# Scaling the attention's probabilities on ScalarE, and moving convolution taps from the V products into the first attention steps

## The reference, cut to what matters

```python
h = rms_norm_2(x, mix_norm_g[l])
u = h @ w_in[l]                                    # 512 columns for the convolution, then q, k, v
c = conformer_conv(conv_in, ...)                   # 31 taps by token, 256 channels
a = dilated_attention(qkv[0], qkv[1], qkv[2], positions)          # 12 heads of 64, 256 keys
mixed = jnp.concatenate([rms_norm_2(c, conv_out_g[l]), rms_norm_2(a, attn_out_g[l])], axis=-1)
x = x + mixed @ w_out[l]
x = x + memory_cross_attention(h, m, w_xq[l], w_xk[l], w_xv[l], w_xo[l])   # 4 heads of 256, 256 keys

def conformer_conv(conv_in, dw_w, dw_b, ln_g, ln_b):
    c = a * jax.nn.sigmoid(gate)
    c = <depthwise convolution with 31 taps>(c) + dw_b
    c = layer_norm(c, ln_g, ln_b)
    return jax.nn.silu(c)
```

## Time and profile before

| what | value |
|---|---|
| median of 3 runs | 2212.12 us (2212.11 to 2212.88) |
| the profiled execution | 2211.59 us, its span 2209.8 us |
| TensorE busy | 1968.7 us, 89% of the span |
| VectorE busy | 1119.8 us, 51% |
| ScalarE busy | 885.3 us, 40% |

### The profile page before, as it was taken

How to read it: one execution, slowest core, us unless ns; L and a number is a source line. 1 busy time by engine, 2 the same in 40 slices (tenths; PEclk the granted TensorE clock), 3 DMA queues, 4 the chain that set the end, 5 groups by cost and what they waited for, 6 DMA issues and landing times.

```text
span 2209.8 us, 33856 instructions
## 1 busy us (share of the span) xinstructions
PE 1968.7 (89%) x14272; PEld 1597.1 (72%) x14272; DVE 1119.8 (51%) x1832; ACT 885.3 (40%) x1504; POOL 16.9 (1%) x31
## 2 busy tenths in 40 slices
PE   6899889999999999989899999998899967667666
PEld 4787667777777877889599999897698754444443
DVE  2344656664887778447655566669665211101111
ACT  2423336554765667444444444643564200000001
POOL 0000000000000000000000000000000000000000
PEclk9899999999999999989999999999899988888898
DMA  7222005453455554224045445443134999999995
GB/s 271 82 77 80 16 6 178 150 184 110 153 181 181 191 177 162 90 69 168 3 155 189 156 159 178 162 156 127 48 117 175 416 420 421 420 419 420 420 420 241
DMA packets 90976, 428.00 MB, mean 194 GB/s; under 512 B 11073, under 2 KB 12610, under 8 KB 65858
## 3 DMA queue, kind: packets, MB, share of 16 engines
q1 hardware_dynamic: 78578, 379.03, 45.6%
q10 hardware_dynamic: 12240, 46.74, 6.2%
HBM read 424.68 MB, written 1.05 MB: 193 GB/s over the span
## 4 chain that ended last, share of the span: by engine, by line
PE 65%; DMA 18%; DVE 9%; ACT 6%; issue 2%; POOL 0%; SPq 0%; DVEq 0%; ACTq 0%
PE bank L458 42%; DMA area<-in_w 7%; PE bank L1532 7%; DMA ring<-in_w 4%; DMA his<-in_w 4%; DMA PPT<-in_w 2%; PE bank L482 2%; PE bank L2383 2%; PE bank L2339 2%; DVE ring_r L437 1%; DVE st L1239 1%; ACT his_r L429 1%; ACT PPT L1187 1%; ACT H L822 1%; PE bank L1170 1%
## 5 line engine op out<-in xcount | busy, mean ns | idle before, releaser
L458 PE MATMUL bank<-HH_r,his_r 128*128 128x256 f32 (+1 forms) x1568 | 532.9, 340 | 19.8 <-issue 9.5
L458 PE MATMUL bank<-HH_r,ring_r 128*128 128x256 f32 (+1 forms) x1568 | 518.5, 331 | 0.0
L437 DVE TENSOR_TENSOR ring_r<-ring,his_r 128x1024 fp32r<-128x1024 f32 x306 | 373.7, 1223 | 274.0 <-ACT his_r L429 272.9
L458 PE MATMUL bank<-H_r,his_r 128*128 128x256 f32 (+1 forms) x1504 | 499.2, 332 | 0.0
L429 ACT ACTIVATE his_r<-ring 128x1024 fp32r<-128x1024 f32 x306 | 323.3, 1058 | 405.9 <-PE bank L458 258.7
L458 PEld LDWEIGHTS bank<-HH_r,his_r 128*128 128x128 f32 x1568 | 298.2, 190 | 60.3 <-issue 16.0
L458 PEld LDWEIGHTS bank<-HH_r,ring_r 128*128 128x128 f32 x1568 | 298.2, 190 | 27.7
L458 PEld LDWEIGHTS bank<-H_r,his_r 128*128 128x128 f32 x1504 | 286.1, 190 | 30.8 <-issue 2.6
L2355 DVE TENSOR_TENSOR tmp<-tmp,bank 128x128 f32<-128x128 f32 x64 | 18.4, 287 | 382.3 <-ACT tmp L2348 265.0
L1532 PE MATMUL bank<-VT_r,his_r 128*128 128x512 f32 (+1 forms) x352 | 122.3, 348 | 9.5 <-DVE YF_r L1308 4.8
L2339 PE MATMUL bank<-area,KF 128*32 128x128 f32 x1888 | 88.2, 314 | 38.4 <-DMA area<-in_w 36.2
(11 more groups left out here) (393 smaller groups left out, 3259.6 us busy)
## 6 DMA issues: line engine op xcount, KB each, us to landing
area<-in_w SPq DMA_DIRECT2D x91, 1024.0 KB, 27.2
ring<-in_w_in SPq DMA_DIRECT2D x102, 512.0 KB, 3.5
ring<-in_w_gate_up SPq DMA_DIRECT2D x88, 512.0 KB, 3.5
ring<-in_w SPq DMA_DIRECT2D x36, 1024.0 KB, 27.4
HH<-in_w SPq DMA_DIRECT2D x26, 1024.0 KB, 27.2
ring<-in_w_down SPq DMA_DIRECT2D x44, 512.0 KB, 3.5
KX<-in_w_mod_rows ACTq DMA_DIRECT2D x28, 512.0 KB, 3.5
VX<-in_w_mod_rows ACTq DMA_DIRECT2D x28, 512.0 KB, 3.5
```

What stands on the lines that cost most here:

```text
L437: ve.eng.tensor_tensor(lo_slot(u), stream.slot(u), hi_slot(n).bitcast(F32), ALU.subtract).then_inc(*ve_lo.up(n))
L458: ins = pe.eng.matmul(out, a, b, start=k == 0 and m == 0, stop=end)
```

## The change

Five things change.

1. In attentions with `ahead=2`, ScalarE scales the probabilities of head h-1 by the reciprocal of their sum, behind the exponentials of head h. VectorE only makes the reciprocal. TensorE's turn waits for ScalarE.
2. The V products' units get one tap each (13 to 18), and steps 0 to 3 of the attention three each (19 to 30), ahead of the low part.
3. What follows the convolution stands two steps later: centre 4 and 5, affine 10, sigmoid 11, squares of the branch 11, its sums 12, its root 13. Its reciprocal stands in step 14, the spread and the gains behind the last step, in a call for h = 15.
4. ScalarE runs one small exponential before the attention.
5. The bank of the spread is given back in step 10, that of the branch after h = 15.

```diff
@@ -1153,7 +1153,7 @@
                             kc = 2 * j + cc_
                             for qb in range(2):
                                 i = qb if c.wide else 0
-                                pe.wait_ge(*ve_soft.at("p", c.site, g, i, c.n - 1))
+                                pe.wait_ge(*(ac_soft if c.ahead == 2 else ve_soft).at("p", c.site, g, i, c.n - 1))
                                 c0 = kc * P if c.wide else qb * 256 + kc * P
                                 ins = pe.eng.transpose(out[:, cc_ * 256 + qb * P:cc_ * 256 + (qb + 1) * P],
                                                        c.pps[slot * c.nq + i][:, c0:c0 + P], ident)
@@ -1187,6 +1187,13 @@
                             ac.eng.activation(p[:, m * w:(m + 1) * w], src[:, m * w:(m + 1) * w], ACT.Exp,
                                               bias=st[:, so + m:so + m + 1], scale=c.rq(h, i + m) if c.rq else 1.0,
                                               accum_out=st[:, so + 4 + m:so + 5 + m]).then_inc(*ac_soft.up("exp", c.site, h, i, m))
+                if c.ahead == 2 and 1 <= h <= c.nh:
+                    slot = (h - 1) % 3
+                    p, r = c.pps[slot], st[:, 8 * slot + 6:8 * slot + 8]
+                    ac.wait_ge(*ve_soft.at("inverse", c.site, h - 1, 0))
+                    for m in range(c.n):
+                        ac.eng.activation(p[:, m * 256:(m + 1) * 256], p[:, m * 256:(m + 1) * 256], ACT.Identity,
+                                          scale=r[:, m:m + 1]).then_inc(*ac_soft.up("p", c.site, h - 1, 0, m))
                 if 0 <= h - c.ahead < c.nh:
                     g = h - c.ahead
                     for j in range(c.nk // 2):
@@ -1216,6 +1223,8 @@
             p, so, w = c.pps[slot], 8 * slot, 512 // c.n
             ve.wait_ge(*ac_soft.at("exp", c.site, h, i, c.n - 1))
             ve.eng.reciprocal(st[:, so + 6:so + 6 + c.n], st[:, so + 4:so + 4 + c.n]).then_inc(*ve_soft.up("inverse", c.site, h, i))
+            if c.ahead == 2:
+                return
             ve.wait_ge(*ve_soft.last())
             for m in range(c.n):
                 ve.eng.tensor_scalar(p[:, m * w:(m + 1) * w], p[:, m * w:(m + 1) * w], st[:, so + 6 + m:so + 7 + m], None,
@@ -1813,7 +1822,7 @@
             for j in range(3):
                 for u in (16 + 2 * j, 17 + 2 * j):
                     ve_split(ve, two_on(unit("w_in_2", 0, 8 * u)))
-                    ve_conv_taps(ve, 2 * u - 19, 2 * u - 17)
+                    ve_conv_taps(ve, u - 3, u - 2)
 
 
         def ve_last_norm(ve, k):
@@ -1864,22 +1873,22 @@
                 if k == 7:
                     for tb in range(2):
                         banks.give("xv", half, tb)
-            if h == 2:
+            if h == 4:
                 out = banks.take((ve_taps, ("centered", 1)), "center")
                 pe.wait_ge(*banks.emptied("center"))
                 pe.wait_ge(*ve_taps.at("tap", 30, 1))
                 for j in range(2):
                     ins = pe.eng.matmul(out[:, 0:N], ones[:, :], CB[:, j, :], start=j == 0, stop=j == 1)
                 ins.then_inc(*pe_sums.up("center"))
-            if h in (4, 10):
-                site = "spread" if h == 4 else "branch"
+            if h in (6, 12):
+                site = "spread" if h == 6 else "branch"
                 pe_open(pe, site)
                 for n in range(2):
                     pe_sum(pe, site, n, 2, N)
-            if h in (7, 13):
-                pe_spread(pe, "spread" if h == 7 else "branch", N, give=False)
-            if h in (8, 14):
-                banks.give("sum", "spread" if h == 8 else "branch")
+            if h in (9, 15):
+                pe_spread(pe, "spread" if h == 9 else "branch", N, give=False)
+            if h == 10:
+                banks.give("sum", "spread")
             if h == 4:
                 pe_open(pe, "attn_out", (ve_norm, ("used", "attn_out")))
             if h in (6, 8, 10, 12, 14):
@@ -1893,41 +1902,41 @@
                     for tb in range(2):
                         ac.eng.activation(VM[:, tb, n // 8 * 512:n // 8 * 512 + 512], banks.ap("xv", n // 8, tb),
                                           ACT.Copy).then_inc(*ac_out.up("xv", n // 8, tb))
-            if h == 3:
+            if h == 5:
                 for n in range(2):
                     ac.wait_ge(*ve_taps.at("centered", n))
                     ac_square(ac, "spread", n, CB[:, n, :], N)
-            if h in (5, 11):
-                ac_sqrt(ac, *(("spread", 2, N, 256, 1) if h == 5 else ("branch", 2, N, 256)))
-            if h == 8:
+            if h in (7, 13):
+                ac_sqrt(ac, *(("spread", 2, N, 256, 1) if h == 7 else ("branch", 2, N, 256)))
+            if h == 10:
                 for j in range(2):
                     ac.wait_ge(*ve_taps.at("shifted", j))
                     ac.eng.activation(tmp[2 + j][:, 0:N], CB[:, j, :], ACT.Exp, scale=-1.0).then_inc(*ac_out.up("branch", j))
-            if h == 9:
+            if h == 11:
                 for n in range(2):
                     ac.wait_ge(*ve_taps.at("gated", n))
                     ac_square(ac, "branch", n, CB[:, n, :], N)
 
         def ve_beside(ve, h):
+            if h < 4:
+                ve_conv_taps(ve, 19 + 3 * h, 22 + 3 * h)
             for n in value_steps(h):
                 ve_split(ve, two_on(value_unit(n)))
-            if h < 2:
-                ve_conv_taps(ve, 25 + 3 * h, 28 + 3 * h)
-            if h == 3:
+            if h == 5:
                 ve.wait_ge(*pe_sums.at("center"))
                 for j in range(2):
                     ve.eng.scalar_tensor_tensor(CB[:, j, :], banks.ap("center")[:, 0:N], -1.0 / 256, CB[:, j, :], ALU.mult,
                                                 ALU.add).then_inc(*ve_taps.up("centered", j))
-            if h == 6:
+            if h == 8:
                 ve_reciprocal(ve, "spread", N)
-            if h == 8:
+            if h == 10:
                 r = spread_out(ve, "spread", N)
                 for j in range(2):
                     ve.eng.scalar_tensor_tensor(CB[:, j, :], CB[:, j, :], vv("ln_g", j), r, ALU.mult,
                                                 ALU.mult).then_inc(*ve_norm.up("used" if j else ("gain", j), "spread"))
                     ve.wait_ge(*ve_norm.last())
                     ve.eng.tensor_scalar(CB[:, j, :], CB[:, j, :], vv("ln_b", j), None, ALU.add).then_inc(*ve_taps.up("shifted", j))
-            if h == 9:
+            if h == 11:
                 for j in range(2):
                     t = tmp[2 + j][:, 0:N]
                     ve.wait_ge(*ac_out.at("branch", j))
@@ -1937,9 +1946,9 @@
                     ve.eng.reciprocal(t, t).then_inc(*ve_taps.up("sigmoid", j))
                     ve.wait_ge(*ve_taps.last())
                     ve.eng.tensor_tensor(CB[:, j, :], CB[:, j, :], t, ALU.mult).then_inc(*ve_taps.up("gated", j))
-            if h == 12:
+            if h == 14:
                 ve_reciprocal(ve, "branch", N)
-            if h == 14:
+            if h == 15:
                 r = spread_out(ve, "branch", N)
                 ve_gains(ve, "branch", CB, 2, "conv_out", MX, r)
 
@@ -1976,6 +1985,8 @@
 
         def pe_mixed(pe):
             pe_attend(pe, dilated, pe_beside)
+            pe_beside(pe, 15)
+            banks.give("sum", "branch")
             pe_sum(pe, "attn_out", 5, 6, N, slots=pair_squares)
             pe_key(pe, 6)
             pe_spread_both(pe)
@@ -2007,6 +2018,7 @@
             banks.give("sum", "attn_out")
 
         def ac_mixed(ac):
+            ac.eng.activation(st[:, 41:42], epsc[:, 0:1], ACT.Exp)
             ac_attend(ac, dilated, ac_beside)
             ac_sqrt_table(ac, 3, 6)
             ac_sqrt(ac, "attn_out", 6, N, 768)
@@ -2029,6 +2041,7 @@
 
         def ve_mixed(ve):
             ve_attend(ve, dilated, ve_beside)
+            ve_beside(ve, 15)
             r = rsts.ap("attn_out")
             ve.wait_ge(*ac_norm.at("sqrt", "attn_out"))
             ve.eng.reciprocal(r[:, 2:4], r[:, 0:2]).then_inc(*ve_norm.up("rstd", "attn_out"))
```

## The result

Median 2226.09 us (4 runs, 2225.47 to 2227.59) against 2212.11 us before (4 runs on the same chip): ratio 1.0065, 95% interval 1.0047 to 1.0082, so 14.0 us slower. I forecast 2216.8 with a range of 2210.5 to 2221.5. The sign was the likelier one, the forecast of 4.7 us was a third of what was measured.

What follows compares the result with a forecast made beforehand. VectorE's taps bound the V products, a VectorE-ScalarE ring the dilated attention, TensorE the memory attention. Terms -0.7 to head 11's reciprocal, +2.1 tail, +2.3 clock, +1.0 memory attention gave +4.7: 2216.8 us, range 2210.5 to 2221.5.

Steps and rivals of the forecast that it cites:

- The scaling's price: A scaling pair on ScalarE costs 0.80 us (0.70 to 1.01), paid nine times in steps 3 to 11: +7.2.
- Steps 0 to 2: Dilated attention's first steps: taps fill VectorE's waits, table load covered; -1.3 and -2.3, then -1.6, then -0.4 us.
- Step 3: Dilated attention: six taps behind the output's low half are paid (+2.4) but cover a wait (-0.6): +1.8 us.
- The early exponential: Ahead of the dilated attention: the table load moves behind the last V eviction and is fully covered, -1.3 us.
- Rival C: Scalings hidden behind waits for TensorE's values: faster, -2.5 us, or -5.6 (2206.5) at best; chance 0.10.
- The tail: Head 11's reciprocal to first product behind attention: ScalarE's file of work +2.1 us, TensorE's half clock +2.3.
- Rival B: Same mechanism as the forecast, but TensorE's clock holds in the tail: +2.4 us, 2214.5; chance 0.35.
- The centre, the affine and the sigmoid only change steps: zero in sum: Dilated attention: moving this work to later steps costs nothing net up to the last reciprocal, 0 us.
- Rival D: Banks held later make scores wait for an output's low half, four at 0.9: +8.3 us, 2220.4; chance 0.10.
- V stage: V products ahead of the attention: twelve taps leave VectorE, mask 0 then waits for scores, -1.9 us (to 0).
- The products behind the tail: Weight products behind the attention start slow at half clock: +1.7 us at the range's upper end, not summed.
- Memory attention: TensorE waits for probabilities scaled on ScalarE, +0.8 first and a little later: +1.0 us (0.5 to 2).

Runs made afterwards that it cites:

- e1: The kernel before, with only the scalings moved to ScalarE in both attentions: ratio 1.0043, +9.3 us.
- e2: The change with the scaling left on VectorE, so only the moves, against the kernel before: ratio 1.0029, +5.7 us.
- e8: The kernel before plus the early exponential, and six taps of steps 0 and 1 ahead of the low part: ratio 0.9970, 2204.57 us.
- e11: e8 with centre, squares, spread, sigmoid and branch two steps later, banks too; scaling on VectorE: ratio 1.0013 to the kernel before.
- e3: The kernel before, with scalings on ScalarE in the dilated attention alone: ratio 1.0033, +6.7 us.
- e5: The kernel before, with the early exponential alone: ratio 0.9994, 2209.93 us.
- e6: The change, with the centre's bank held until step 6 and the spread's until step 11: ratio 1.0061 to the kernel before.
- e9: The change, with the spread's bank alone given back in step 11 instead of 10: ratio 1.0058 to the kernel before.
- e12: e8 plus an early exponential ahead of the memory attention too: 2203.31 us, ratio 0.9966 to the kernel before.
- e13: e8 with the sigmoid and the branch alone two steps later: ratio 1.0016 to the kernel before.
- e4: The kernel before, with scalings on ScalarE in the memory attention alone: ratio 1.0004, +1.7 us.
- e7: The change, with the branch's spread and gains put behind the first weight product: 2223.13 us, ratio 1.0054 to the kernel before.

## Why the prediction was wrong in size, step by step

**Where the miss lies.** In my sum the scalings make +9.2 (0.8 in step 1, -0.6 in step 2, 7.2, 0.8 in the tail, 1.0), and the moves the rest, -4.5. The scalings alone measured +9.3 (e1), the moves alone +5.7 (e2). So the whole miss is in the moves. By the ratios the part of them that e8 has gained 0.30%; the later steps then cost 0.43% (e11 against e8), the twelve taps brought over 0.16% (e2 against e11), the scalings 0.36% (the change against e2).

**Right.** *The scaling's price*, 0.80 a pair: measured 0.78 to 0.80 in each of the steps 8 to 11 of e3. *Steps 0 to 2*: -3.6, -1.6, -0.4 forecast; measured -3.62, -1.58, -0.50. Step 2 is right by luck: the wait that I let the six taps fill goes without them too (2.05 us in e11, 2.32 in e8, against 4.26). *Step 3*: +1.8 and its scaling pair, 2.6 forecast; measured +1.88. *The early exponential*, -1.3: measured 1.28 in e5's step 0. The Trainium skill (ScalarE: Activation LUTs, "What ACT_TABLE_LOAD costs") has 2.66 us for load and drain together; here the trace differs, for this kernel got back 1.28, the load's own duration. *Rival C* (scalings hidden) is refuted by e1 and e3. *The tail*: +2.1 and +2.3 for the clock forecast up to the first product behind the attention, measured +4.14, with the granted clock at 0.50 from 1618 to 1624. From the last scaling pair to the eviction ScalarE took 6.58 us (forecast 4.7 at full and 7.0 at half clock), and in it waited 0.99 and 0.89 for TensorE: the clock's term is 1.9, not 2.3. Rival B (the clock holds) did not come. That the tail's scaling pair cost its 0.8 isn't shown: it does in e1 (8.93 against 8.13), but e11 has 12.48 without it where the change has 12.27.

**The term that failed: "The centre, the affine and the sigmoid only change steps: zero in sum".** I had put it at nothing without a reason, and in the steps of the change it misses some 3 us. Rival D rested on "No row shows such a wait". None of my rows did, but the trace before has TensorE's turn 3.46 us behind the affine in step 8 (shown above), just where the 6 us at 0.50 begin that I did read the earlier trace rows. By my own terms step 6 should have taken 4.7 + 0.8 = 5.5 and step 10 6.34 + 1.6 (the affine) + 0.8 = 8.7; they took 6.98 and 10.55. That is D's mechanism, two waits for a bank, though by VectorE's centre and affine; the wait for an output's low half came in e6 and e9. e9 shows that the 1.85 in step 10 are that wait, but also that taking it away gains next to nothing in the whole: the end was 1.46 longer. So the bank waits show that the term is not zero; they do not by themselves account for the loss.

e11 against e8 is the cleaner test of the term. The later steps without any scaling cost some 10 us there, where the term and the tail's without its scaling pair allow 0 + 3.6: 4.0 more up to the last reciprocal (2.5 against e12, by the chance of step 7) and 5.8 in the end.

e13 puts the seat at the branch. The sigmoid adds 4.9 in step 11 but frees only 2.8 in step 9, because TensorE's half clock behind the affine's wait stood under it and comes to light when it leaves. Mask 10 then waits 2.06 us for TensorE; that the clock alone makes these is argued from the profiles of e13 and e11, not tried by itself. And the end grows by 7.3. I had read that stretch at 0.50 and had asked only what it does to the tail, not what the sigmoid covered where it was. Why the end grows by 5.8 in e11 and 7.3 in e13, where I had 3.6, is open but for the 1.5 to 1.7 behind the tail (below). In the change itself step 9 did give the whole 4.9 (9.10 to 5.01 with the scaling's 0.8 in it), so there the first of these is not part of the 14.

**V stage, -1.9 forecast, +0.6 measured.** The reading of who ends last was right (the chain above), the size was not. TensorE sets the pace now, so its clock decides. In each of the 14 profiles TensorE waits 2.62 us just ahead of these products, in the same place, and then starts them at a granted clock that differs by execution (by four taps a unit I mean four instructions):

```
matmuls in the first 4 us (clock)   four taps a unit: start to mask 0       two taps a unit
35, 36 (1.00)                       19.66 before, 19.67 e4, 19.66 e13        -
26, 27 (0.71, 0.72)                 19.68 e3, 19.72 e5                       18.88 e6
22, 23 (0.58 to 0.61)               20.25 e1, 20.25 e8, 20.25 e12            19.42 e9, 19.93 e2
20 (0.50)                           21.37 e11                                20.28 after, 20.75 e7
```

At like clock (the same row of the table) two taps instead of four are worth 0.3 to 1.1 us, not 1.9; with four taps VectorE covers a cold start down to the second line of the table. No halved kernel was caught at full clock, so whether the 1.9 would be had there stays open. And the twelve taps that left are paid where they went: 4.1 us in steps 2 and 3 (e2 against e11), so this move lost some 3 us. The Trainium skill (TensorE: Matmul & The Clock Gate, "Why this matters for your kernels") warns of idle gaps between bursts of matmuls, but of longer ones than this. The trace has the lower level behind the shorter gap too: in 11 of 14 profiles the clock was below 1.00 behind the 2.62 us, and in 3 it was not.

**The products behind the tail, 0 forecast, +1.5 measured.** I had priced it at 1.7 as the upper end of the range ("slow products") and left it out of the sum. TensorE idles 3.17 us ahead of them now, and 1631 to 1635 ran at 0.57. By the clock it is the mechanism of the term that I did count.

**Memory attention, +1.0 forecast, +2.0 measured**, the upper end. e1 and e4 have the same 2.0, e2 and e3 none: it is the scaling's. I had counted the first turn fully and the later ones at next to nothing; three of them wait.

**Not in the prediction: +1.1 behind unit xo.** The work there is unchanged. In all kernels looked at TensorE is busy 2.83 of 5 us in one window, and the next one ran at 0.50 (after, e9), 0.66 (before, e2) or 1.00 (e7). With e7's 2.7 us in the other direction, that is the clock after a stretch that the edits don't touch. The change, e6 and e9 have 39.8 us in this stretch, and all ten others beside e7 have 38.6 to 38.9. That looks less like chance than like the time at which these three arrive, but no run tried it.

The sum of the misses is 2.5 (V) + 3.0 (steps) - 0.3 (tail) + 1.5 + 1.0 + 1.1 = 8.8; with the forecast's 4.7 that makes 13.5, against 13.66 in the profile and 14.0 by the medians.

## What to carry to other kernels

When a block of side work is moved later, ask what it covered where it stood, and what is left to cover it at the end: here twelve taps (in steps 0 and 1) put ahead of a wait and a table load moved forward gave 7.6 us alone, while the sigmoid and the branch moved towards the last head cost more than that. An operation that hides in one engine's idle time is not free on the other if that one's work is in the ring: two instructions of 0.35 us hidden on VectorE became 0.80 us paid on ScalarE in steps 8 to 11, and 6.5 us from mask 0 to the last reciprocal (e3). And a rotated bank is a wait in disguise: before moving its reader by a step, look for TensorE's waits for that reader in the trace that you have (here 3.46 us), list which product comes round to the bank next, and what stands ahead of the reader in its queue.

## What the runs showed of the hardware that I had not expected

The same wait of TensorE, 2.62 us at the same place of the program, was followed by granted clocks of 0.50, 0.58 to 0.61, 0.71 and 1.00 in different executions, and the 4 us behind it held 20 to 36 matmuls. With four taps a unit the stretch to mask 0 took 19.66 to 21.37 us by it, so a single profile of such a stretch can't price an edit to within 1.5 us.

The two halves of the change added up within what the medians can tell, 9.3 + 5.7 = 15.0 for 14.0, although both lengthen the same ring of engines.
